# Ten layer norms of a four-layer network: worked by token tile, normalized values turned, g and b applied when the turned values are evicted

## The reference, cut to what matters

```
def layer_norm(h, g, b):
    mu = mean(h); var = mean(square(h - mu))        # over the 1024 features of a token
    return (h - mu) * rsqrt(var + 1e-5) * g + b

# block one, for l in 0, 1
h = layer_norm(ALPHA * h + token_mixer(h, ...), ln1_g[l], ln1_b[l])
h = layer_norm(ALPHA * h + peer_ffn(h, ...),    ln2_g[l], ln2_b[l])
# block two, for l in 0, 1
x = layer_norm(ALPHA * x + hybrid_mixer(x, ...),           ln_g[l,0], ln_b[l,0])
x = layer_norm(ALPHA * x + memory_cross_attention(x, ...), ln_g[l,1], ln_b[l,1])
x = layer_norm(ALPHA * x + square(relu(x @ w_up)) @ w_down, ln_g[l,2], ln_b[l,2])
```

## Time and profile before

| | |
|---|---|
| median of three runs | 3476.33 us |
| profiled execution | 3471.35 us |
| its span in the trace | 3468.2 us |
| PE busy | 3199.4 us (92%) |
| DVE busy | 1772.8 us (51%) |
| ACT busy | 1146.6 us (33%) |
| mean granted PE clock | 0.945 of full |

### The profile page before, as it was taken

One profiled execution on the slowest core, in us unless ns is written; L12 is line 12 of the kernel. 1 busy time (PEld: TensorE's weight loads), 2 busy tenths in 40 slices (PEclk: granted clock), 3 DMA queues, 4 the chain that ended last, 5 costly groups with the idle time before them and its releaser, 6 DMA issues.

```text
span 3468.2 us, 52680 instructions
## 1 busy us (share of the span) xinstructions
PE 3199.4 (92%) x19658; PEld 2701.5 (78%) x19658; DVE 1772.8 (51%) x3549; ACT 1146.6 (33%) x1728; POOL 1.8 (0%) x6
## 2 busy tenths in 40 slices
PE   8889899999998889999999998899977989998698
PEld 6578689898987658779899896777647878675597
DVE  1367964787463339774687656022224531322346
ACT  1312344444442311244444443022213421230343
POOL 0000000000000000000000000000000000000000
PEclk9999999999999989999999999979978998998799
DMA  4234255544554223244544554322223543123244
GB/s 184 79 134 147 74 193 182 194 146 170 182 193 159 98 106 138 97 158 182 192 160 148 191 183 180 134 73 86 97 109 133 187 177 122 61 86 122 97 182 158
DMA packets 68004, 493.46 MB, mean 142 GB/s; under 512 B 7560, under 2 KB 7568, under 8 KB 8336
## 3 DMA queue, kind: packets, MB, share of 16 engines
q1 hardware_dynamic: 67552, 490.42, 39.1%
q0 software_dynamic: 304, 1.06, 0.1%
HBM read 490.39 MB, written 1.06 MB: 142 GB/s over the span
## 4 chain that ended last, share of the span: by engine, by line
PE 88%; DVE 6%; issue 3%; ACT 2%; DMA 1%; DVEq 1%; SPq 0%; POOL 0%; ACTq 0%; POOLq 0%
PE ps L228 14%; PE ps L563 8%; PE ps L564 8%; PE ps L565 8%; PE ps L238 8%; PE ps L536 7%; PE ps L537 7%; PE ps L538 7%; PE ps L254 3%; PE ps L245 3%; PE ps L1400 2%; PE ps L812 1%; PE ps L1316 1%; DVE hots L1112 1%; PE ps L269 1%
## 5 line engine op out<-in xcount | busy, mean ns | idle before, releaser
L626 DVE TENSOR_TENSOR ring_l<-ring,tile_h 128x1024 fp32r<-128x1024 f32 x576 | 679.8, 1222 | 599.9 <-ACT tile_h L583 599.7
L583 ACT ACTIVATE tile_h<-ring 128x1024 fp32r<-128x1024 f32 x576 | 577.2, 1051 | 452.9 <-PE ps L565 452.9
L536 PE MATMUL ps<-x_h,tile_h 128*128 128x256 f32 x2048 | 586.2, 286 | 14.8 <-DVE ring_l L626 14.8
L537 PE MATMUL ps<-x_l,tile_h 128*128 128x256 f32 x2048 | 580.4, 283 | 0.0
L538 PE MATMUL ps<-x_h,ring_l 128*128 128x256 f32 x2048 | 580.3, 283 | 0.0
L228 PE MATMUL ps<-xT,ring 128*128 128x256 f32 x2048 | 459.6, 387 | 12.9 <-DVEq L1524 4.4
L228 PEld LDWEIGHTS ps<-xT,ring 128*128 128x128 f32 x2048 | 396.8, 195 | 72.0 <-issue 14.9
L536 PEld LDWEIGHTS ps<-x_h,tile_h 128*128 128x128 f32 x2048 | 394.1, 192 | 15.8 <-issue 15.6
L537 PEld LDWEIGHTS ps<-x_l,tile_h 128*128 128x128 f32 x2048 | 394.2, 192 | 0.2
L538 PEld LDWEIGHTS ps<-x_h,ring_l 128*128 128x128 f32 x2048 | 393.8, 192 | 0.0
L563 PE MATMUL ps<-tile_h,w_even 128*128 128x512 f32 x640 | 251.5, 393 | 15.0 <-DVE w_even L648 15.0
(11 more groups left out here) (274 smaller groups left out, 3754.0 us busy)
## 6 DMA issues: line engine op xcount, KB each, us to landing
ring<-stream SPq DMA_DIRECT2D x464, 1024.0 KB, 4.8
cs<-consts SPq DMA_DIRECT2D x1, 1712.5 KB, 8.6
x<-x_in SPq DMA_DIRECT2D x1, 1024.0 KB, 5.2
arena<-scratch POOLq DMA_DIRECT2D x1, 1024.0 KB, 6.0
out<-x SPq DMA_DIRECT2D x1, 1024.0 KB, 4.0
tab<-table SPq DMA_DIRECT2D x1, 1.0 KB, 8.5
scratch<-arena POOLq DMA_DIRECT2D x1, 12.0 KB, 1.8
```

Of the source, the lines that this page charges most:

```text
L536: nc.tensor.matmul(out, uh[:, c, f], x_h[:, c, :], start=(c == 0), stop=False)
L537: nc.tensor.matmul(out, uh[:, c, f], x_l[:, c, :], start=False, stop=False)
L583: nc.scalar.activation(tile_h[:, j % 2, n], slot(k + j)[:, n], ACT.Copy).then_inc(hi_ready, 1)
L626: nc.vector.tensor_tensor(low_of(k + j)[:, n], slot(k + j)[:, n], tile_h[:, j % 2, n].bitcast(F32), ALU.subtract).then_inc(lo_ready, 1)
```

## The change

1. The tile that closes an accumulation is ordered by tokens: token tile 0 is complete (banks 0 and 1) when half the tile's matmuls are done, and `acc_first` says so. In the split form, `pe_down_block` orders its last tile likewise.
2. `dve_norm` works one token tile after the other. The residual of tile 0 and its moments come ahead of the wait for the end of the accumulation; each tile has its own root, and its normalization is done in two halves of 512 features, each of which releases four turning matmuls (`ln_half`).
3. PE turns the normalized values, without g and b. ACT evicts them in 16 ACTIVATEs of 128x128, and since features are partitions then, applies g and b as scale and bias (`gb`, copied from the layer's small tile). VectorE applies g and b to `x` itself afterwards; it waits for the turning (`xt_mm`), since it overwrites what PE reads. `act_norm` starts with a root of a constant.
4. The first tile behind a norm waits chunk by chunk for the evictions (`up_as_turned`). The slot of the norm's tile, and the small or keys tile's, are released in the middle of its second half, where PE waits for the norm's last adds. `tile_done` runs one tile later accordingly.
5. The MLP's first tile is computed as `up_as_turned`, in plain f32, from `xT`; the other 15 stay split.
6. Block two's padding tile moves from the end of the layer to behind the projections. The output is stored in two halves.

The diff, cut to its core (`...` marks what is left out):

```diff
 A_TILES = A_LN2 + 1
-A_TILES += -A_TILES % SLOTS
...
 B_PROJ = 1
-B_CMP = B_PROJ + 12
+B_PAD = B_PROJ + 12
+B_CMP = B_PAD + 1
...
-SPLIT_B = 2 * MLP_PAIRS
+SPLIT_B = 2 * MLP_PAIRS - 1
...
-            eng.wait_ge(tile_done, base + 4 * i + (k + 1))
+            eng.wait_ge(tile_done, base + 4 * i + (k + 2))
...
+        def down_by_tokens(w, lhs, first):
+            for tt in range(TT):
+                for j in range(2):
+                    for half in range(2):
+                        last = nc.tensor.matmul(ps[2 * tt + half][:, :], lhs(j, tt),
+                                                w[:, j * D + half * 512:j * D + half * 512 + 512],
+                                                start=(first and j == 0), stop=(j == 1))
+                if tt == 0:
+                    last.then_inc(acc_first, 1)
+            return last
+
+        def up_as_turned(pe, m, w, bank, release):
+            for fb in range(2):
+                for c in range(KC):
+                    if fb == 0:
+                        pe.wait_ge(xt_ready, 2 * KC * m + (KC + c + 1))
+                    if fb == 1 and c == KC // 2:
+                        release()
+                    last = nc.tensor.matmul(ps[bank][:, fb * SEQ:(fb + 1) * SEQ], w[:, c, fb * P:(fb + 1) * P],
+                                            xT[:, c, :], start=(c == 0), stop=(c == KC - 1))
+            return last
+
+        def norm_read(pe, n):
+            pe.wait_ge(ln_x, n * TT + TT)
+            pe.sem_inc(tile_done, 1)
...
-        def act_turn_x(act, m):
-            for tt in range(TT):
-                for g in range(2):
-                    act.wait_ge(xt_mm, m * 4 + (2 * tt + g + 1))
-                    nc.scalar.activation(xT[:, 4 * g:4 * g + 4, tt * P:(tt + 1) * P],
-                                         ps[4 + 2 * tt + g][:, :].rearrange("p (j n) -> p j n", j=4),
-                                         ACT.Copy).then_inc(xt_ready, 1)
+        def act_turned(act, m, tt, first, last, which=None):
+            for c in range(first, last):
+                if c % 4 == 0:
+                    act.wait_ge(xt_mm, m * 4 + (2 * tt + c // 4 + 1))
+                to, src = xT[:, c, tt * P:(tt + 1) * P], ps[4 + 2 * tt + c // 4][:, c % 4 * P:(c % 4 + 1) * P]
+                if which is None:
+                    ins = nc.scalar.activation(to, src, ACT.Copy)
+                else:
+                    ins = nc.scalar.activation(to, src, ACT.Identity, bias=gb[:, which, 1, c:c + 1],
+                                               scale=gb[:, which, 0, c:c + 1])
+                ins.then_inc(xt_ready, 1)
+
+        def act_norm(act, n, which):
+            def root(tt):
+                act.wait_ge(ln_var, n * TT + (tt + 1))
+                nc.scalar.activation(std[:, tt:tt + 1], mv[:, tt, 1:2], ACT.Sqrt,
+                                     bias=cs[:, CONST["eps"]][:, 0:1]).then_inc(ln_std, 1)
+            nc.scalar.activation(warm[:, :], cs[:, CONST["ones"]][:, 0:1], ACT.Sqrt)
+            root(0)
+            act_turned(act, n + 1, 0, 0, 6, which)
+            root(1)
+            act_turned(act, n + 1, 0, 6, KC, which)
+            act_turned(act, n + 1, 1, 0, KC, which)
...
+            dve.wait_ge(acc_first, n + 1)
+            residual(0, 0)
+            step.after(residual(0, 1))
+            moments(0)
             finished(dve, block, l, k - 1)
...
+            residual(1, 0)
+            normalize(0)
+            step.after(residual(1, 1))
+            moments(1)
+            normalize(1)
             arrived(dve, block, l, k)
+            dve.wait_ge(ln_half, n * 2 * TT + 2 * TT)
+            for tt in range(TT):
+                dve.wait_ge(xt_mm, 4 * n + (4 + 2 * tt + 2))
                 last = nc.vector.tensor_tensor(x[:, tt, :], x[:, tt, :], slot(k)[:, 0:D], ALU.mult)
...
+                order = [(b, tt) for tt in range(TT) for b in range(2)] if closes else \
+                    [(b, tt) for b in range(2) for tt in range(TT)]
...
+                    if closes and (b, tt) == (1, 0):
+                        ins.then_inc(acc_first, 1)
...
-            pe.wait_ge(small_read, l + 1)
-            pe.sem_inc(tile_done, 1)
-            pe.wait_ge(xt_ready, l * 8 + 4)
-            for j in range(6):
+            arrived(pe, 1, l, A_PROJ)
+            up_as_turned(pe, 2 * l, chunks(A_PROJ), 4, small_and_norm_read).then_inc(tile_done, 1)
+            for j in range(1, 6):
...
+            arrived(pe, 2, l, B_PAD)
+            pe.sem_inc(tile_done, 1)
...
-            g, s = LAYERS * PAIRS + l * MLP_PAIRS, LAYERS * SPLIT_A + l * SPLIT_B
-            pe_up_block(pe, B_MLP, s, g, LAYERS + l)
+            g, s = LAYERS * PAIRS + l * MLP_PAIRS, LAYERS * SPLIT_A + l * SPLIT_B - 1
+            arrived(pe, 2, l, B_MLP)
+            pe.wait_ge(u_act, g + 1)
+            up_as_turned(pe, norm + 2, chunks(B_MLP), 4, lambda: norm_read(pe, norm + 2)).then_inc(tile_done, 1)
+            pe.wait_ge(xl_ready, LAYERS + l + 1)
+            for j in range(1, 4):
+                pe_up(pe, B_MLP, s, g, 0, j)
...
-                    sp.wait_ge(tile_done, 4 * g + (s - 3))
+                    sp.wait_ge(tile_done, 4 * g + (s - 2))
...
+            for tt in range(TT):
+                sp.wait_ge(ln_x, all_norms * TT + (tt + 1))
+                sp.dma_start(out[tt * P:(tt + 1) * P, :], x[:, tt, :]).then_inc(stored, 16)
```

More of the change, by code:

```diff
@@ L293, in dve_norm @@
         def dve_norm(dve, step, n, block, l, k):
-            finished(dve, block, l, k - 1)
-            for tt in range(TT):
-                for half in range(2):
-                    h = x[:, tt, half * 512:(half + 1) * 512]
-                    last = nc.vector.scalar_tensor_tensor(h, h, ALPHA, ps[2 * tt + half][:, :], ALU.mult, ALU.add)
-            step.after(last)
-            for tt in range(TT):
-                for half in range(2):
-                    last = nc.vector.bn_stats(st[:, tt, half, :], x[:, tt, half * 512:(half + 1) * 512])
@@ L314, in dve_norm, with halves, residual, moments @@
-            step.after(last)
-            arrived(dve, block, l, k)
-            for tt in range(TT):
+            def halves(tt, half):
+                return x[:, tt, half * 512:(half + 1) * 512]
+            def residual(tt, half):
+                h = halves(tt, half)
+                return nc.vector.scalar_tensor_tensor(h, h, ALPHA, ps[2 * tt + half][:, :], ALU.mult, ALU.add)
+            def moments(tt):
+                nc.vector.bn_stats(st[:, tt, 0, :], halves(tt, 0))
+                step.after(nc.vector.bn_stats(st[:, tt, 1, :], halves(tt, 1)))
+                carry_wait()
+                nc.vector.bn_aggr(mv[:, tt, :], st[:, tt, :, :]).then_inc(ln_var, 1)
@@ new lines, in normalize @@
+            def normalize(tt):
+                dve.wait_ge(ln_std, n * TT + (tt + 1))
+                step.after(nc.vector.reciprocal(rstd[:, tt:tt + 1], std[:, tt:tt + 1]))
+                for half in range(2):
+                    h = halves(tt, half)
+                    nc.vector.tensor_scalar(h, h, mv[:, tt, 0:1], rstd[:, tt:tt + 1], ALU.subtract, ALU.mult)\
+                        .then_inc(ln_half, 1)
+            dve.wait_ge(acc_first, n + 1)
+            residual(0, 0)
+            step.after(residual(0, 1))
```

162 lines of the change are left out of this document (87 added, 75 removed).

## The result

The changed kernel takes 3378.44 us (median of 4 runs, 3376.28 to 3380.17) where the kernel before takes 3476.6 on the same chip: a ratio of 0.9718, 95% interval 0.9691 to 0.9745. One of the four runs of the kernel before was slow (3511.39 us) and is not in the ratio; without it its median is 3476.33. The forecast was 3378. The profiled execution spans 3376.2 us, 92.0 under the 3468.2 of before; the medians lie 98.2 apart, since the profiled run of before took 5 us less than its median.

What follows compares the result with a forecast made beforehand. A strict chain of waits through each norm, in which PE idled 11.25 us, was taken as the bound; TensorE holds 88%. Places sum to 98.0 us off 3471.35, so 3373, and 3378 against the median 3476.33; range 3358 to 3401.

Steps and rivals of the forecast that it cites:

- four plain norms: After both w_o and both mix products: first tile evicted at T+15.1, not T+24.9 (T: accumulation's end); 39.2 us.
- two layer ends: Norms ending a layer, one per block, before the loop's jump: first tile evicted at T+17.1, was 25.9; 17.6 us.
- two MLPs: Norms before the MLP: a plain first tile fills PE's idling, second tile starts at T+16.4, was T+29.84; 26.8 us.
- the table: Norm followed by the position table's way through DRAM: ACT's copy earlier, PE's waits and low clock gone; 11.4 us.
- the end: Last norm: adds of b end at T+10.7 for 12.3, and the store goes out by halves; 3.0 us.
- The early start: At each norm, the closing tile's first half is ready 3.4 us early (split tiles 2.6 to 2.7), so VectorE starts then.
- The chain of the norm: After T at a plain norm: second root T+4.2, second turning T+5.2, next tile's first matmul T+6.7.
- (a): ACT becomes the norm's bound, with an eviction costing 600 ns: 20 us at nine norms, 3398 us; 14%.
- (b): The clock stays low through the first tile as before, despite shorter idles: 8 us less gain, 3386 us; 13%.
- (c): Clock never falls for a first tile, waits inside cost nothing, evictions little over 277 ns: 11 more, 3367 us; 8%.
- (d): The early start fails because something holds VectorE until the whole tile is done: 29 us less gain, 3407; 3%.
- (e): Slower than before: the late slot release starves PE of loads at nine norms, 3495 us; 3%.

Runs made afterwards that it cites:

- the held kernel: The changed kernel with VectorE held at each norm until the whole closing tile is done: 3412.74 us, ratio 0.9831.

## Why the prediction was right

By its steps, in time from T to the eviction or start named there:

| term | forecast, us | measured, us |
|---|---|---|
| four plain norms: first tile evicted at T+15.1 | 4 x 9.8 = 39.2 | T+15.63, 15.65, 15.10, 15.10: 38.2 |
| two layer ends: T+17.1 | 2 x 8.8 = 17.6 | T+18.54, 18.62: 14.7 |
| two MLPs: second tile from T+16.4, the part 13.4 shorter | 26.8 | T+16.07; the parts 13.52 and 13.54 shorter: 27.1 |
| the table: T+32.2 | 11.4 | T+31.41: 12.2 |
| the end | 3.0 | 2.6 |
| sum | 98.0 | 94.8 |

The sum of the places is 94.8 and the span 92.0 shorter, with 0.7 won before the first norm: 3.5 us are lost in between. The two largest losses are clock, 1.6 us in each expert block and 1.7 in a token mixer; elsewhere some of it comes back. In each expert block a low stretch stands behind a piece of 3.20 us in which PE waits for VectorE's `w_even` (793.6 to 796.8 in the first), each time at the same distance from T. Before had the same idle piece and no low stretch behind it. First before, then the changed kernel:

```profile
807.30:810.70 3.40, 2.91 (x13) 2.42 (x14) 3.40 (x4) 1.24 (x2) 0.00 (x0) 1.00 0.46 195
```

```profile
798.20:801.40 3.20, 3.20 (x9) 2.44 (x8) 3.20 (x4) 0.22 (x1) 0.00 (x0) 0.50 0.01 3
```

In the token mixer behind the first layer end a low stretch of 3.4 us became one of 6.8. Again before, then the changed kernel, at the same distance from the next T:

```profile
1137.50:1140.60 3.10, 1.06 (x5) 0.73 (x5) 1.73 (x8) 2.01 (x9) 0.00 (x0) 0.99 0.55 225
```

```profile
1122.50:1125.90 3.40, 3.17 (x8) 2.25 (x9) 1.19 (x6) 0.44 (x2) 0.00 (x0) 0.50 0.02 5
```

The forecast of 3378 against the median held to 0.4 us. That is partly luck: the sum was 6 us too high for the profiled pair, and the 5 us between the profiled run of before and its median were not there in the changed kernel.

Step by step. *The early start* came as worked out (3.40 us for 3.4; at split tiles 2.7), and the run that takes it away cost 33.4 for 29: the size was short, as the first turning then falls into the low clock as well. *The chain of the norm* was right within 0.4: second root at T+4.20 for 4.2, second turning at 5.35 for 5.2, first matmul at 7.11 for 6.7. The half-width normalizations were too cheap in the sum: two in a row took 1.00 for 0.8, and PE starts 0.6 behind the start of one, for 0.4. Half the width is not half the time. The low clock and the waits inside it cost the first tile of a plain norm 1.3 to 1.6 us, for 1.5. *The eviction* took 467 ns for my 430, the next 0.35 later for 0.36. The Trainium skill, "ScalarE: Activation LUTs", section "What ACT_TABLE_LOAD costs", with its 93 ns for each [128,1] operand, gave 479 as an estimate worked out from its figures, and was nearer than mine. The trace agrees with it: without the two operands an eviction took 283 ns, 92 less for each. The run without them shows that it made no difference to the time here. *The layer ends* are the step that failed in size: the jump was put at 2.2 and the start at T+9.1; it took 2.4 to 3.1 behind the turning and the start was T+9.65 to 9.73, and the tile took 8.9 us for 8.0, at the low clock first. I had given the low clock 0.9 there; with the jump PE idles 2.8 and then 2.4 to 3.1 us, broken only by the second turning, and the tile takes what it took before the change (8.9). *The MLP* came within 0.15 per part: PE waited 1.22 for 1.3. *Table and end* held within 0.8; at the table the 1.5 for entering the loop did not come, as PE goes from the flips into the tile without idling.

*The rivals.* (a) is refuted by the evictions at 283 ns that won nothing. (b) in its strict form is refuted: the first tile of a plain norm takes 8.5 where it took 9.5, and behind the sixteen blocks turned at one go 7.5. That also goes against the rule weighed, in the Trainium skill's "TensorE: Matmul & The Clock Gate", "Part 4: PE-mode transpose": by it those sixteen blocks would do nothing for the clock. There PE was idle from 183.5 to 192.7 and then did nothing but turn them, and the clock stands at 0.95 over the tile behind them. The cleaner proof is still the one before the change, where the clock came up with PE idle behind the turning. (b) is right of the layer ends, where the tile takes 8.9 us as before. (c) was wrong: the clock does fall. (d) is what the held kernel does, and it is not what the changed one does. (e), slots that are freed late, shows nowhere: a load lands in 4.8 us as before, and PE waits for none of the stream's loads after the start.

```profile
ring<-stream SPq DMA_DIRECT2D x464, 1024.0 KB, 4.8
```

The removals add up to more than the gain: 33 for the early start, 38 for g and b, 24 for the tile that follows the evictions chunk by chunk, 19 for the plain first MLP tile make 114 for 92. So they can't be read as shares. Part of the surplus is clock, as each removal makes PE idle for longer; how much was not measured.

Open: why the jump costs more behind this norm (2.4 to 3.1 us) than before (2.2). It is no fixed price: with g and b ahead of the turning it took 1.2 and 1.5. Open too is why layer ends and the stretch behind them differ by up to 4.5 us between kernels that are alike there, with the low clock beginning up to 3.4 us sooner or later. Taking the jump away was not tried.

## What to carry to other kernels

Cut a chain that several engines share by halves, so that one engine's second half runs beside another's first, and take off it what the next stage can do without. Both were needed here: one wait of 11.3 us became two of 1.4 and 2.8, but with g and b back in the halved chain it was one of 9.3 again. Scale and bias belong where the data is moved anyway, if that engine has room. Work a gain out to the next busy stretch and not only to the place where it arises: a microsecond or two won at each norm vanished in most of the runs here that sought one, in a wait or a low clock a tile later, and only a run with many rounds beside the same kernel told it from a gain.

## What the runs showed of the hardware

- An idle piece is paid for twice. PE starting 2.34 us later made the tile end 2.9 to 4.7 us later, as the clock was at 1.2 GHz for longer.
- Filling the idle pieces with matmuls of constants keeps the granted clock at 1.00 through a norm, even with 1.44 us of idling left in it, but an idle piece of 1.9 us behind it then brought 3.4 us of low clock to a busy stretch that had had the full one. Filling that too removed it. What is won locally by fillers (1.1 to 1.9 us at six norms) did not show in the time.
- The same stretch of the same kernel does not always get the same clock. The part before the first norm is alike in all these kernels and took from 179.0 to 183.4 us; the changed kernel's two profiles have it at 180.7 and 183.1. Most of that lies in the program's first tile, whose matmuls took 379 ns in the one and at first 634 in the other: the tile took 7.17 and 9.14 us. From there to the end they agree within 0.1 us (3195.5 and 3195.6).
- VectorE's normalization of 128x512 takes 0.54 us where that of 128x1024 takes 0.81; in a row, two halves take 1.00 and two whole ones 1.53. So halving a tile to overlap costs 0.2 to 0.3 us each time.
